# A decoder layer step: DMA order and early loads in the three memory stages

## The reference, cut to what matters

```
y  = ssd_recurrent(...)              # sample rows: state = exp(dt*A)*state + x*dt*B ; y = sum(state*C)
ys = rmsnorm((y + d_skip*xs) * silu(z))            # the sample's right half of "mixed"
x  = x + concat(rmsnorm(attn), ys) @ w_out         # "mixed" @ w_out, 2048 -> 1024
mk, mv = rmsnorm(mem) @ w_mk, rmsnorm(mem) @ w_mv  # 256 memory rows
x  = x + softmax(rmsnorm(x) @ w_mq @ mk.T) @ mv @ w_mo
x  = x + peer_ffn(rmsnorm(x))                      # gathers of experts, the long last stage
```

## Time and profile before

| | us |
|---|---|
| median of the runs | 4473.97 (4469.43 to 4479.78) |
| the profiled execution's own time | 4475.78 |
| its span, first to last instruction | 4474.0 |
| stage with the sample's step, about | 1096 to 1190 |
| memory_read, about | 1190 to 1365 |
| memory_read_sample, about | 1365 to 1508 |
| expert stage | 1508 to 4474 |

### The profile page before, as it was taken

The page is one execution under the profiler, slowest core; times in us unless marked ns, Lnnn a source line. Parts: engine busy times, 40 slices in busy tenths (PEclk is TensorE's granted clock), DMA queues, the critical chain, the costliest instruction groups (busy, mean ns, idle before and its releaser), DMA issues.

```text
span 4474.0 us, 42016 instructions
## 1 busy us (share of the span) xinstructions
PE 3857.5 (86%) x11661; PEld 1983.1 (44%) x11661; DVE 2497.8 (56%) x5480; ACT 1289.9 (29%) x3847; POOL 1362.9 (30%) x1243
## 2 busy tenths in 40 slices
PE   8998689997797799998889999889999888887776
PEld 4555244553362355553345554345554344433332
DVE  2333256554412376754586764487765468766664
ACT  2333022322011032342333342233334233333332
POOL 0000033330000133444433444433344333334443
PEclk9896799998897899999999999999999999999999
DMA  6001000002703499999999999999999999999997
GB/s 210 28 28 36 30 15 19 14 14 87 293 15 142 178 418 418 419 417 420 421 402 406 416 420 420 421 419 389 411 419 412 421 419 405 419 418 400 419 420 294
DMA packets 227374, 1316.68 MB, mean 294 GB/s; under 512 B 27240, under 2 KB 43661, under 8 KB 93488
## 3 DMA queue, kind: packets, MB, share of 16 engines
q0 software_dynamic: 148608, 1082.20, 58.5%
q1 hardware_dynamic: 77416, 232.21, 13.8%
q10 hardware_dynamic: 1152, 0.00, 0.0%
HBM read 1283.71 MB, written 32.68 MB: 294 GB/s over the span
## 4 chain that ended last, share of the span: by engine, by line
PE 26%; DMA 26%; DVE 7%; issue 3%; ACT 2%; DVEq 1%; ACTq 0%; POOL 0%; POOLq 0%
DMA ex_ring<-in_expert_uv,ex_idx 25%; PE psum L2757 17%; DVE ex_ring L3142 4%; PE psum L2786 4%; PE psum L2735 3%; ACT ex_diag L2938 1%; PE psum L2805 1%; DMA pair_p<-scratch_mixed 1%; PE psum L2830 0%; ACT ex_weight L2933 0%; DMA ex_ring<-in_expert_uv,ex_idxT 0%; PE psum L2847 0%; POOL ex_ring L2677 0%; DVE ex_top_at L3037 0%; DVE ex_top_at L3049 0%
## 5 line engine op out<-in xcount | busy, mean ns | idle before, releaser
L2757 PE MATMUL psum<-ex_ring,ex_diag 128*128 128x512 f32 x4096 | 1922.2, 614 | 330.0 <-ACT ex_diag L2938 306.3
L3142 DVE CUSTOM_DVE_ANT_0 ex_ring<-ex_ring,ex_x_rows 128x1024 f32<-128x1024 f32 x1024 | 1251.0, 1226 | 818.6 <-DMA ex_ring<-in_expert_uv,ex_idx 752.5
L2677 POOL DMA_INDIRECT ex_ring<-in_expert_uv,ex_idx x1024 | 1146.5, 1120 | 1743.0 <-PE psum L2757 1537.9
L2757 PEld LDWEIGHTS psum<-ex_ring,ex_diag 128*128 128x128 f32 x4096 | 773.8, 195 | 1301.5 <-issue 852.5
L2929 ACT ACTIVATE ex_dots<-ex_dots 128x2 f32<-128x2 f32 x512 | 104.1, 203 | 1792.4 <-DVEq L3145 1792.0
L2938 ACT ACTIVATE ex_diag<-ident,ex_weight 128x128 f32<-128x128 f32 x1024 | 355.0, 393 | 36.1 <-issue 0.7
L1063 PE MATMUL psum<-w_zx,ssd_hT 128*128 128x512 f32 (+1 forms) x768 | 296.2, 542 | 23.7 <-DVEq L1492 22.9
L2735 PE MATMUL psum<-ex_xT,ex_chunk 128*128 128x256 f32 (+1 forms) x1280 | 276.4, 360 | 4.2 <-ACT ex_sub L2914 2.9
L2735 PEld LDWEIGHTS psum<-ex_xT,ex_chunk 128*128 128x128 f32 x1280 | 229.0, 191 | 97.8 <-issue 77.2
L2933 ACT ACTIVATE ex_weight<-ex_gates,ex_dots 128x1 f32<-128x1 f32 x1024 | 246.1, 287 | 36.3 <-issue 1.1
L1063 PEld LDWEIGHTS psum<-w_zx,ssd_hT 128*128 128x128 f32 x768 | 138.0, 193 | 179.9 <-issue 156.1
(11 more groups left out here) (457 smaller groups left out, 3721.3 us busy)
## 6 DMA issues: line engine op xcount, KB each, us to landing
ex_chunk<-in_route_wq SPq DMA_DIRECT2D x80, 512.0 KB, 7.9
ex_chunk<-in_w_out SPq DMA_DIRECT2D x48, 512.0 KB, 9.1
ex_ring<-in_expert_uv,ex_idx POOLq DMA_INDIRECT x1024, 20.4
ex_chunk<-in_read_wq SPq DMA_DIRECT2D x24, 512.0 KB, 7.9
ex_chunk<-in_w_mo SPq DMA_DIRECT2D x24, 512.0 KB, 8.0
w_zx<-in_w_in SPq DMA_DIRECT2D x1, 10304.0 KB, 35.7
w_out<-in_w_out SPq DMA_DIRECT2D x2, 4096.0 KB
w_out<-in_cache_mem_k SPq DMA_DIRECT2D x8, 1024.0 KB, 13.3
```

The costliest lines, as they stand in the source:

```text
L2677: nc.gpsimd.indirect_dma_start(out=ring[:, n % RING, :], out_offset=None, in_=io["expert_uv"], in_offset=bass.IndirectOffsetOnAxis(ap=idx[ ...
L2757: ins = nc.tensor.matmul(psum[c][:], diag[:, q % 3, s, :], ring[:, n % RING, D + c * BANK:D + (c + 1) * BANK], start=(n % SLOTS == 0), sto ...
L3142: nc.vector.tensor_tensor_reduce(ring[:, n % RING, 0:D], ring[:, n % RING, 0:D], x_rows[:, tile % 3, :], 1.0, 0.0, ALU.mult, ALU.add, dots ...
```

## The change

The DMAs and waits of three stages are written in another order, two loads are moved to an earlier stage, and buffers are handed through.

- Step stage: the readback of `step_y` is issued in front of the second half of w_out. The store of the scaled rows is issued in front of p_mem_v. ScalarE squares `step_y` between its copies for the first and the second 128 rows of mv; VectorE scales in front of its four copies to mkT.
- The first 128 rows of "mixed" and the 8 rows of x_sample are loaded in the step stage, behind w_mv, into buffers that now live through all three stages (`mixed`; the sample's x goes straight into `x1`).
- memory_read: no first load of "mixed"; the FFN gain is loaded behind w_mo, and VectorE waits for it only where it is first used. When the second block is turned, the 8 sample rows of "mixed" are loaded into `mixed[0:8]`.
- memory_read_sample: its two loads are gone; it waits for `own_in` at 32 instead.

```diff
 # memory_kv_and_sample_step, SP
+            sp.dma_start(mixed_rows[:], io["mixed"][0:P, :]).then_inc(rows_in, 16)
+            sp.dma_start(own_x[:], io["x_sample"]).then_inc(own_in, 16)
             sp.wait_ge(state_ready, 1)
...
-            sp.dma_start(w_out[:, DB:2 * DB, :], w_out_rows[:, DB:2 * DB, :]).then_inc(w_out_in, 16)
             sp.wait_ge(pairs_stored, 16)
             sp.dma_start(y[:], io["rows3"]).then_inc(y_in, 16)
+            sp.dma_start(w_out[:, DB:2 * DB, :], w_out_rows[:, DB:2 * DB, :]).then_inc(w_out_in, 16)
             sp.wait_ge(k_ready, MT)
             sp.dma_start(io["p_mem_k"].rearrange("(m p) n -> p m n", p=P), mk[:]).then_inc(stored, 16)
+            sp.wait_ge(out_ready, 1)
+            sp.dma_start(io["mixed"][SEQ:TOKENS, D:2 * D], y[:]).then_inc(out_stored, 16)
             sp.wait_ge(v_ready, MT)
             sp.dma_start(io["p_mem_v"].rearrange("(m p) n -> p m n", p=P), mv[:]).then_inc(stored, 16)
-            sp.wait_ge(out_ready, 1)
-            sp.dma_start(io["mixed"][SEQ:TOKENS, D:2 * D], y[:]).then_inc(out_stored, 16)
 # ScalarE
             for m in range(MT):
+                if m == 1:
+                    act.wait_ge(gated, 1)
+                    nc.scalar.activation(junk[0:DEC, :], y[:], ACT.Square, accum_out=yms[:]).then_inc(yms_ready, 1)
                 act.wait_ge(projected, 4 + 2 * m + 2)
...
-            act.wait_ge(gated, 1)
-            nc.scalar.activation(junk[0:DEC, :], y[:], ACT.Square, accum_out=yms[:]).then_inc(yms_ready, 1)
 # VectorE
             nc.vector.tensor_tensor(y[:], y[:], gates[:], ALU.mult).then_inc(gated, 1)
+            dve.wait_ge(yrstd_ready, 1)
+            nc.vector.tensor_scalar(y[:], y[:], yrstd[:], None, ALU.mult).then_inc(out_ready, 1)
             for m in range(MT):
...
             dve.drain()
-            dve.wait_ge(yrstd_ready, 1)
-            nc.vector.tensor_scalar(y[:], y[:], yrstd[:], None, ALU.mult).then_inc(out_ready, 1)
 # memory_read, SP
-            load_mixed(0)
             load_x(0)
-            sp.dma_start(gain_ffn[:], io["norm_ffn_w"].broadcast_to([P, D])).then_inc(gain_in, 16)
             sp.dma_start(w_mq[:], io["w_mq"].rearrange("(b p) n -> p b n", p=P)).then_inc(w_mq_in, 16)
+            sp.sem_inc(mixed_in.sem, 16)
             load_mixed(1)
             sp.dma_start(w_mo[:], io["w_mo"].rearrange("(b p) n -> p b n", p=P)).then_inc(w_mo_in, 16)
+            sp.dma_start(gain_ffn[:], io["norm_ffn_w"].broadcast_to([P, D])).then_inc(gain_in, 16)
             load_x(1)
+            sp.wait_ge(mixed_turned.sem, mixed_turned.last(READ))
+            sp.dma_start(mixed[0:DEC, :], io["mixed"][SEQ:TOKENS, :]).then_inc(own_in, 16)
 # TensorE: turn_mixed(0) waits for rows_in; VectorE:
+                if t == 0:
+                    dve.wait_ge(gain_in, 16)
                 dve.wait_ge(rstd2_ready.sem, rstd2_ready.this(t))
...
-            dve.wait_ge(gain_in, 16)
             mixed_rows(0)
 # memory_read_sample
-            sp.dma_start(mixed[:], io["mixed"][SEQ:TOKENS, :]).then_inc(loaded, 16)
-            sp.dma_start(x[:], io["x_sample"]).then_inc(loaded, 16)
-            pe.wait_ge(loaded, 32)
+            pe.wait_ge(own_in, 32)
```

More of the change, by code:

```diff
@@ L1632, in _, with memory_kv_and_sample_step @@
             nc.vector.tensor_tensor(dt[:], raw[:], neg[:], ALU.add).then_inc(dt_ready, 1)
-def memory_kv_and_sample_step(nc, io, psum, shared, mkT, mv, w_out, w_mo, w_out_in):
+def memory_kv_and_sample_step(nc, io, psum, shared, mkT, mv, w_out, w_mo, own_x, mixed_rows, w_out_in, rows_in, own_in):
     ident, gain = shared["ident"], shared["gain_mem"]
@@ L1811, in _, with memory_read @@
             dve.drain()
-            dve.wait_ge(yrstd_ready, 1)
-            nc.vector.tensor_scalar(y[:], y[:], yrstd[:], None, ALU.mult).then_inc(out_ready, 1)
-def memory_read(nc, io, psum, shared, w_out, w_mq, w_mo, mkT, mv, w_out_in):
+def memory_read(nc, io, psum, shared, w_out, w_mq, w_mo, mkT, mv, mixed, w_out_in, rows_in, own_in):
     ident = shared["ident"]
@@ L1825, in memory_read @@
         sb, sem, event = stage.buffer, stage.semaphore, stage.event
-        mixed = sb("read_mixed", [P, 2 * D])
         x = sb("read_x", [P, D])
@@ L1922, in turn_mixed @@
             def turn_mixed(u):
-                pe.wait_ge(mixed_in.sem, mixed_in.this(u))
+                if u:
+                    pe.wait_ge(mixed_in.sem, mixed_in.this(u))
+                else:
+                    pe.wait_ge(rows_in, 16)
                 turn_blocks("m", mixed, u, 4)
@@ L2159, in _, with memory_read_sample @@
             ffn_rows(READ - 1)
-def memory_read_sample(nc, io, psum, shared, w_out, w_mq, w_mo, x1):
+def memory_read_sample(nc, io, psum, shared, w_out, w_mq, w_mo, x1, mixed, own_in):
     ident = shared["ident"]
@@ L2171, in memory_read_sample @@
         sb, sem = stage.buffer, stage.semaphore
-        mixed, x, junk, q = sb("rs_mixed", [DEC, 2 * D]), sb("rs_x", [DEC, D]), sb("rs_junk", [DEC, D]), sb("rs_q", [DEC, D])
+        junk, q = sb("rs_junk", [DEC, D]), sb("rs_q", [DEC, D])
         mT, hT = sb("rs_mT", [P, 2 * DB, DEC]), sb("rs_hT", [P, DB, DEC])
@@ L2190, in memory_read_sample @@
         v = [places[b % VP] for b in range(DEC)]
-        loaded, turned, mT_ready, summed, x1_ready = (sem("rs_" + n) for n in ("loaded", "turned", "mT_ready", "summed", "x1_ready"))
+        turned, mT_ready, summed, x1_ready = (sem("rs_" + n) for n in ("turned", "mT_ready", "summed", "x1_ready"))
         x1_turned, hT_ready, ms_ready, rstd_ready, projected, q_ready = (
@@ L2331, in _ @@
             ins.then_inc(mT_ready, 1)
-            dve.wait_ge(loaded, 32)
+            dve.wait_ge(own_in, 32)
             dve.wait_ge(summed, 1)
@@ L2335, in _ @@
                 cols = slice(c * BANK, (c + 1) * BANK)
-                ins = nc.vector.tensor_tensor(x1[:, cols], psum[1 + c][0:DEC, :], x[:, cols], ALU.add)
+                ins = nc.vector.tensor_tensor(x1[:, cols], psum[1 + c][0:DEC, :], x1[:, cols], ALU.add)
             ins.then_inc(x1_ready, 1)
@@ L3404, in program @@
             ssd_sample_inputs(nc, io, psum, shared, w_zx)
-        w_out_in = nc.alloc_semaphore("w_out_in")
+        w_out_in, rows_in, own_in = (nc.alloc_semaphore(n) for n in ("w_out_in", "mixed_rows_in", "own_rows_in"))
         mkT, mv = sb("mkT", [P, DB, N_MEM]), sb("mv", [P, N_MEM // P, D])
@@ L3411, in program @@
             w_mo = memory.enter_context(nc.sbuf_tensor("w_mo", [P, DB, D], F32))
-            memory_kv_and_sample_step(nc, io, psum, shared, mkT, mv, w_out, w_mo, w_out_in)
+            mixed = memory.enter_context(nc.sbuf_tensor("read_mixed", [P, 2 * D], F32))
+            memory_kv_and_sample_step(nc, io, psum, shared, mkT, mv, w_out, w_mo, x1, mixed, w_out_in, rows_in, own_in)
             w_mq = memory.enter_context(nc.sbuf_tensor("w_mq", [P, DB, D], F32))
-            memory_read(nc, io, psum, shared, w_out, w_mq, w_mo, mkT, mv, w_out_in)
-            memory_read_sample(nc, io, psum, shared, w_out, w_mq, w_mo, x1)
+            memory_read(nc, io, psum, shared, w_out, w_mq, w_mo, mkT, mv, mixed, w_out_in, rows_in, own_in)
+            memory_read_sample(nc, io, psum, shared, w_out, w_mq, w_mo, x1, mixed[0:DEC, :], own_in)
         expert_mix(nc, io, psum, shared, mkT, mv)
```

## The result

The changed kernel took 4464.66 us (median of 9 runs, 4455.93 to 4469.23), the kernel before beside it 4471.19 (9 runs, 4462.38 to 4479.78): ratio 0.9981 [0.9972, 0.9990] (95% interval), 6.5 us less by the medians, 4.5 to 12.5 by the interval: small, but clear of no change. In a later measurement it was 4462.79 (11 runs) against 4473.47 (15 runs), 0.9975 [0.9966, 0.9984]: 10.7 us less by the medians. The forecast of 4463.4 holds; the sum behind it was 10.6, and one of its three terms had the wrong sign.

The account below looks back on a forecast made before the run. The expert stage was taken as bound by its gathers, the three changed stages by waits. Terms of 0.7 + 6.6 + 3.3 = 10.6 us off 4474.0 gave 4463.4 us, range 4456 to 4472.

Parts of the forecast that it names:

- Head of memory_read: At memory_read's start, rows already loaded save 4.6 us and no wait for the gain 2.0: 6.6 us.
- Head of the sample stage: At memory_read_sample's start, TensorE finds its data at the barrier and starts with VectorE: 3.3 us saved.
- Early loads: Two loads moved into the step stage behind w_mv, about 0.4 us an issue: no cost.
- Step stage: The reordered step stage ends at 1189.2 instead of 1189.9: 0.7 us saved, bounds +2.9 to -1.1.
- the queue sets the end ... 1189.2: Step stage: w_out's half lands at 1184.4, then p_mem_k 2.34, the store 0.1 and p_mem_v 2.34 us later.
- the hole: Step stage: the queue is empty when w_out's half is issued behind the readback, so it lands 2.2 us later.
- the slot I gave it: Step stage: w_out's second half is issued at 1171.93, where p_mem_k was issued before.
- The rule of the Trainium skill that I weighed: A transfer has about 2.0 us fixed beside its bytes; by it the sum would be about 11.5 us.
- The readback doesn't get ahead: Rival: step_y's readback lands behind w_out's half, the step stage ends 5.4 us later: 4469.5; chance 0.13.
- The expert stage gives it back: Rival: the expert stage's mean rate falls from 404 to 401 GB/s, 22 us more: 4485.8; chance 0.06.
- The clock rises earlier: Rival: unbroken turning ahead of memory_read's products brings TensorE's clock rise earlier, 2.4 us more saved: 4461.0; chance 0.12.
- The sum: Whole kernel: 0.7 + 6.6 + 3.3 = 10.6 us saved.

Follow-up runs that it names:

- gain_only: The kernel before with only the FFN gain's load moved behind w_mo and VectorE's wait moved to its first use: 4469.52 us, one run.
- own_only: The kernel before with only the sample's x and rows loaded ahead, as in the change: 4469.80 us, one run.
- before_third: The kernel before, with no edit, traced a third time: 4476.71 us.
- k_early: The changed kernel with p_mem_k stored as soon as it is there, ahead of the wait for the state: 4455.23 us, ratio 0.9966.
- piece_in_hole: k_early's kernel with 1 MB of w_out's second half issued ahead of the wait for the stored pairs: 4453.02 us, ratio 0.9961.
- after_again: The changed kernel once more, with no edit: 4462.79 us.
- reorder_only: The kernel before with only the step stage's new order, no early loads: 4467.57 us, ratio 0.9994.
- small_between: The changed kernel with one more load of 8 rows between w_out's second half and p_mem_k's store: 4463.61 us, one run.
- k_in_hole: The changed kernel with p_mem_k's store issued ahead of the wait for the stored pairs: 4461.68 us, ratio 0.9981.
- prefetch_only: The changed kernel with the step stage's old order, early loads and both new heads kept: 4463.93 us, ratio 0.9983.

## Why the prediction was right, step by step

**Head of memory_read: 6.6 forecast, 6.5 measured.** From the memset to the first product it is 13.1 to 13.5 us in the six traces with both loads late, 6.7 in the seven with the change's head. 2.2 of it are the gain's wait (gain_only; I had 2.0), 4.3 the rows (I had 4.6), by the difference of the two heads.

**Head of the sample stage: 3.3 forecast, 3.4 measured** (3.4 to 0.04), by own_only alone. That it reaches the stage's end needs two traces whose clock ran alike, since TensorE works at either of two clocks (granted 0.50 and 1.00). Timelines of before_third and then k_early, in both of which the first products took 30.0 us:

```profile
1366.13 0.95 POOL L2315 MEMSET rs_blank<- 120x1024 f32 x1 [5.17 <-POOLq L127]
1371.84 30.04 PE L2251 MATMUL psum<-w_out,rs_mT 128*8 128x512 f32 x64 [0.45 <-DVE rs_mT L2328]
...
1509.43 0.10 POOL L2661 MEMSET ex_minus_half<- 128x2 f32 x1 [4.28 <-POOLq L127]
```

```profile
1355.52 0.95 POOL L2321 MEMSET rs_blank<- 120x1024 f32 x1 [5.18 <-POOLq L127]
1357.85 30.00 PE L2257 MATMUL psum<-w_out,rs_mT 128*8 128x512 f32 x64 [0.45 <-DVE rs_mT L2334]
...
1495.34 0.10 POOL L2667 MEMSET ex_minus_half<- 128x2 f32 x1 [4.26 <-POOLq L127]
```

1509.43 - 1366.13 = 143.30, and 1495.34 - 1355.52 = 139.82: 3.5 us, the head's gain whole. All eight rises and falls of the clock in the stage stand 3.5 us earlier in the second (read in windows of half a microsecond). For memory_read such a pair is before (174.8) and piece_in_hole (168.2): the clock rises 4.9 and 4.8 us behind the first product, and all six rises and falls stand 6.5 to 7 us earlier. Their difference is 6.6.

Without choosing pairs: memory_read and memory_read_sample together took 313.4 to 318.3 us (mean 316.7) in the five traces with both old heads, and 305.5 to 308.1 (mean 306.3) in the seven with both new ones. That is 10.5 us, where the heads alone give 9.9.

**Early loads: forecast no cost, measured none** (94.2 and 94.4 us). The reason was half wrong: I had 0.4 us an issue, and SP stood 11.18 us in that of "mixed", with w_mv just issued ahead of it. The gain's load at its new place behind w_mo held SP too, for 7.21 us, where it had taken 0.42; nothing was to be issued behind it for another 23 us. The first was hidden because SP had nothing to issue until the state was ready, and w_mv landed only 0.5 us later (26.4 for 25.9).

**Step stage: -0.7 forecast, +1.5 to +1.8 measured. This term failed, by "the queue sets the end ... 1189.2".** The mechanism was right: the wait for the scaled rows is gone, the readback gets ahead (1.9 us, I had 3), and the queue with its hole comes last. Its size was not. Windows of 1 us of the changed kernel, the hole and then the end of the half of w_out:

```profile
1172.00:1173.00 1.00, 0.73 (x7) 0.50 (x5) 0.00 (x0) 0.00 (x0) 0.00 (x0) 1.00 0.59 204
1173.00:1174.00 1.00, 0.00 (x0) 0.00 (x0) 0.00 (x0) 0.00 (x0) 0.00 (x0) 1.00 0.00 1
1174.00:1175.00 1.00, 0.00 (x0) 0.00 (x0) 0.00 (x0) 0.00 (x0) 0.00 (x0) 1.00 0.43 53
1175.00:1176.00 1.00, 0.00 (x0) 0.00 (x0) 0.57 (x1) 0.00 (x0) 0.00 (x0) 1.00 0.63 123
...
1184.00:1185.00 1.00, 0.00 (x0) 0.00 (x0) 0.00 (x0) 0.00 (x0) 0.00 (x0) 0.50 1.22 348
1185.00:1186.00 1.00, 0.00 (x0) 0.00 (x0) 0.00 (x0) 0.00 (x0) 0.00 (x0) 0.50 0.77 135
```

At 414 GB/s, a usual window of these loads, the first four would have carried 1656 KB; they carried 381, which is 3.1 us lost where I had 2.2. The last two carried 483 KB of 828: 0.8 us lost that my sum didn't have. By the landings: p_mem_v landed 18.8 us behind the issue of w_out's half (1173.90 to 1192.7); I had 12.5 + 2.34 + 0.1 + 2.34 = 17.3. And that issue stands 0.7 us later in its stage than the slot I gave it (76.1 us behind the memset, for 75.4). 1.5 + 0.7 = 2.2 us is the whole way from -0.7 to +1.5. It is outside the bounds I kept: they ran from 2.9 us gained to 1.1 lost, and 1.5 to 1.8 were lost.

Of the 1.5, some 0.4 came from the row that I chose. The 12.5 us of the earlier trace rows are a store, out_s_ssm, whose windows read 492 to 524 GB/s with single ones at 33; the loads run at about 414. The same trace has a load of this very size on an empty queue, w_out's first half, with the store of the pairs behind it. From its timeline and its DMA issues:

```profile
1158.64 0.38 SPq L1694 DMA_DIRECT2D w_out<-in_w_out  x1
1163.65 0.33 SPq L1697 DMA_DIRECT2D scratch_rows<-step_y_pairs  x1
...
scratch_rows<-step_y_pairs SPq DMA_DIRECT2D x1, 32.0 KB, 7.9
```

The pairs landed at 1163.65 + 7.9 = 1171.55, 12.9 us behind the load's issue. Another 0.8 is the fall at the half's end; 0.3 is left over.

The fall has a pattern, though no cause. It shows where a load of w_out was issued to an empty queue and the next large transfer behind it was a store: at the half's end in after, after_again, reorder_only, k_early and small_between, at the end of the first half in k_in_hole. Where the next large transfer was a load (the first half in before, 402 at its end), or the load had come to a busy queue (the half in before, 373 at the lowest; the last 3 MB in piece_in_hole, 401), at most 0.2 us were lost. In between stands k_in_hole's second half, which came to a queue that still carried p_mem_k's bytes and lost 0.4.

The 0.7 us of the later slot were there before the hole: the first half of w_out was issued 62.7 us behind the memset, in after_again 63.0, where before, reorder_only and prefetch_only have 62.1 to 62.4, and the readback follows it by 12.9 to 13.1 us in all of them. That fits the reordering alone giving +1.0 and the whole change +1.5 to +1.8. It hangs on when the store of the state starts and lands. Whether the early loads delay that isn't shown: small_between and piece_in_hole, which have them too, stand at 62.3 and 62.1, and small_between's stage took 96.1 us all the same.

The rule of the Trainium skill that I weighed ("DMA: Bandwidth & Descriptors", section "Anatomy of one DMA — SWDGE (gpsimd) path", the fixed part of about 2.0 us on a landing that is waited for) pointed at the right place, and its figure, for GpSimd's path, the wrong way: by the estimate made from it the sum would have been about 11.5 us, and the stages' lengths give some 8.4. For the hole the rows give 3.1 us, more than the page or I had.

**The rivals.** *The readback doesn't get ahead*: refuted by the row at 1175.43. *The expert stage gives it back*: refuted, 2963.0 to 2967.0 us in all 14 traces, with no relation to when it starts. *The clock rises earlier*: it does in some executions. With the turning unbroken ahead of the products, the rise came 0.5 to 1.1 us ahead of the first product in three traces (after_again, k_early, small_between: 165.7 to 166.1 us in the stage) and 3.1 to 4.8 us behind it in the four others (167.8 to 169.1). In those three the clock rose before any product of the stage, when TensorE had only turned for 3.9 us; I had argued that turning doesn't bring the rise nearer. In the seven traces with the first rows loaded late it never came before 3.1. That it takes the unbroken turning is likely by these counts, and not shown. It is worth some 2 to 3 us of memory_read in part of the executions, but little of it reaches the total: the three traces have 139.8 to 140.0 us in the sample stage, and by both stages together they lie at 305.5 to 306.1, the four others at 306.0 to 308.1.

**The sum.** By what the kernel fixes: -6.5 - 3.4 + 1.5 = -8.4 us, against -6.5 and -10.7 by the medians of the two measurements (8.5 and 11.2 by their ratios). The time was hit in part by luck: the forecast started from 4474.0, the median of three runs, and nine gave 4471.19, 2.8 us lower, while the gain of 6.5 was 4.1 short of 10.6. The two misses offset each other to 1.3 us. The profiled spans differ by 8.2 too, but by another sum: +1.3 ahead of the change, +1.5 step, -6.0 read, -6.0 sample, +0.9 expert. That the two sums agree is chance.

## What to carry to other kernels

A load that a stage needs first, issued one stage earlier where the queue has room, gives back the whole wait at the stage's head. A wait for a landing between two big transfers on the same queue left that queue without 3.1 us of its bytes here; before moving a small transfer ahead of a big one, look for a piece of the big one that can be sent ahead of that wait and for a store that could go earlier still (together 6.2 us off the step stage, in piece_in_hole). A store sent into the same gap gave only 0.4. When you size a transfer by a row, take one of the same direction as well as the same size. For effects of a few microseconds compare a stage from barrier to barrier in both traces, and only between executions with the same clock pattern: the total moves by 10 to 20 us with things the change never touches.

## What the runs showed of the hardware

- The DMA issue that stood directly behind w_mv's held SP for 10.8 to 11.2 us in all eight traces that have one there, 1 MB or 8 rows alike, where SP's big loads otherwise took about 0.4 us. The gain's load behind w_mo held it for 5.7 to 7.3 us in all eight that have it there (0.42 in its old place). Both were covered here; in front of anything urgent they would not be. What makes them long isn't shown.
- With w_out's half begun on an empty queue and a large store behind it, the rate fell not only at its start but also in its last two microseconds (348 and 135 GB/s; in small_between 201 and 340). Where either was missing, at most 0.2 us were lost. Its cause stays open.
- With the same code in memory_read (the seven traces with the new head), the granted clock rose from 0.50 anywhere from 1.1 us ahead of the first product to 4.8 us behind it. In the kernel before, the sample stage took 137.4 us in one trace and 143.3 in three, at mean clocks of 0.85 and 0.81; the rise came 2.7 and 4.9 us behind its first product.
